# Issuing the expert weights of a mixture-of-experts stage from SyncE and ScalarE instead of GpSimd

## The chip, the cores and the metric

The kernel runs on one core of a Trainium2 chip, all in float32. The metric is the device time in microseconds of one execution. It computes one inference step of a decoder layer for a prompt of 512 tokens and a group of 8 samples, 520 tokens in all. Names of engines: PE is TensorE (PEld its weight load), DVE is VectorE, ACT is ScalarE, POOL is GpSimd, SP is SyncE.

## The reference

The layer is: adaLN norm, one input projection, four parallel token mixers, merge, output projection, residual; then a second norm and a mixture of experts. Only the last part matters here:

```python
def moe_ffn(h, lp):                       # x2: (520, 1024)
    scores = sigmoid(x2 @ w_router)       # 64 experts
    # group-limited choice: 4 of 8 groups, then the best 8 experts of a token
    gate = scores[idx] / sum * 2.5
    out = sum over the 8 chosen e of gate_e * swiglu(x, w_gate[e], w_up[e], w_down[e])
    out += swiglu(x, w_sh_gate, w_sh_up, w_sh_down)      # shared expert

def swiglu(x, wg, wu, wd):                # wg, wu (1024, 256), wd (256, 1024)
    return (silu(x @ wg) * (x @ wu)) @ wd
```

Each of the three matrices of an expert is 1 MB, so the 64 experts are 201 MB that come from HBM once.

## The kernel before

Up to some 870 us the kernel does the mixers, the merge and the router. The expert stage begins there and ends at about 1500 us; then the eight rows of each token are read back and added.

**Items, lanes and blocks.** The rows that go to one expert are cut into items of 64 rows. The items, in order of expert, are dealt to six lanes in six consecutive runs. A round `p` takes one item of each lane, and a block `(p, q)`, q = 0 to 2, takes those of lanes 2q and 2q+1: 128 rows, one half with the weights of one expert, the other with those of another. Here there are 16 rounds and so 48 blocks and 96 lane places. If a lane's item has the same expert as its item before, the weights in the lane's buffer are used again and not loaded.

**Buffers.** Each lane has one buffer for gate and up (`wgu`, 2 MB) and one for down (`wdn`, 1 MB), so a block's weights are loaded over those of the block three before. The rows of a block go to `xg[q]`, three buffers too.

**TensorE's order** (`block`, L2569) is: `gate_up` of block i (32 matmuls recorded on L2541), `down` of block i-1 (16, L2566), the transposes of block i's middle rows (2, L2551). `gate_up` waits for the semaphore `wg{q}` to reach 64 for each round (four transfers of 16), and `down` for `wd{q}` to reach 32 for each.

**ScalarE's order** (`block`, L1234): silu of the gate half (L1211), its half of the result copy of block i-1 to `ybuf` (L1224), and the copy of the turned middle rows, `hmT` (L1232), which `down` of block i needs. VectorE multiplies gate and up (L1900), turns the gathered rows of block i+2 into columns (L1917), and copies the other half of the result (L1927).

**GpSimd's order** (`steady`, L856) is one list per block: copy two columns of the order table (L788) after `gu_done` says that the product three blocks before the target is over; issue four indirect gathers of gate and up for block i-1 (`load_gate_up`, L768, recorded on L765); copy four more columns; gather the rows of block i (L779); issue two indirect gathers of down for block i-2 (`load_down`, L774); wait for the result of block i-5 and scatter it to HBM (L783). All eight go into one software queue, `q0`. The index of a weight gather is a row number for each of the 128 partitions, and a lane that needs no load has numbers beyond the bounds check, so that its rows are skipped while the semaphore still counts.

**The first blocks** are written out by hand (L817 to L850), because the buffers of the first six lanes come free one after the other as the stage before ends: some waits (`x1_out`, `sh_gu`, `sh_out0`, `sh_out1`, `sh_y`) stand between the loads.

**SyncE** loads and stores for the rest of the kernel; in the expert stage it stores the five shared-expert results (L598) and then waits for the end, when it loads the results back (L615 on, `early_load`).

Of the kernel before, what the change touches and what calls it, by code (L numbers as in the profile page):

```python
# [18 lines left out]
P = 128  # L19
# [120 lines left out]
def trunk(nc, A, O):  # L140
# [13 lines left out]
    yd = nc.dram_tensor("expert_rows", (TOK * TOPK, D), F32, kind="Internal").ap()  # L154

    with ExitStack() as ctx:
# [189 lines left out]
        last_p = view(TAB + 294, [1], 1, dt=I32)  # L346

# [60 lines left out]
        def rows(t):  # L408
            return P if t < NT else NS
# [8 lines left out]
        def _(sp):  # L418
            def load(dst, src, s):
                sp.dma_start(dst, src).then_inc(sem[s], 16)  # L420
# [181 lines left out]
            for t in range(TILES):  # L602
                sp.wait_ge(sem["sh_row"], t + 1)
                load(shared[t * P:t * P + rows(t), :], sh[t][0:rows(t), :], sh_stored[t])

            sp.wait_ge(sem["r_ready"], 1)
            last = sp.value_load(last_p, min_val=LAST_MIN - 1, max_val=MAXP - 2) + 1
            sp.wait_ge(sem["r_ready"], 3)
# [43 lines left out]
        def _(pool):  # L652
# [109 lines left out]
            w_rows = [A[name][0].rearrange("e (p c) n -> (e p) (c n)", p=P) for name in ("w_exp_gate", "w_exp_up", "w_exp_down")]  # L762

            def weight_rows(dst, src, index, s):
                pool.indirect_dma_start(out=dst, out_offset=None, in_=src, bounds_check=NE * P - 1, oob_is_err=False,  # L765
                                        in_offset=bass.IndirectOffsetOnAxis(ap=index, axis=0)).then_inc(sem[s], 16)

            def load_gate_up(q, at, lanes=range(2)):  # L768

                for lane in lanes:  # L770
                    for m in range(2):
                        weight_rows(wgu[2 * q + lane][:, m, :, :].rearrange("p c n -> p (c n)"), w_rows[m], at[:, lane:lane + 1], f"wg{q}")

            def load_down(q, at, lanes=range(2)):  # L774
                for lane in lanes:
                    weight_rows(wdn[2 * q + lane].rearrange("p c n -> p (c n)"), w_rows[2], at[:, 3 + lane:4 + lane], f"wd{q}")

# [8 lines left out]
            def order_part(p, q, lo, hi):  # L786
                pool.sem_inc(sem["x_col"], 1)
                pool.tensor_copy(order[q][:, lo:hi], orders.rearrange("p s n -> p (s n)")[:, bass.ds(p * 18 + (6 * q + lo), hi - lo)]).then_inc(sem["pool_chain"], 1)  # L788

            def gate_up_order(p, q):  # L790

                pool.wait_ge(sem["gu_done"], p * 3 + q - 3)
                order_part(p, q, 0, 2)
                pool.wait_ge(sem["pool_chain"], p * 6 + (n0 + 2 * q + 1))
                pool.sem_inc(sem["x_col"], 1)

            def rest_order(p, q, end=0):

                i = p * 3 + q
                if end < 3:  # L800
                    pool.wait_ge(sem["x_t"], i - 2)
                pool.wait_ge(sem["dn_done"], i - 4)
                pb, qb = block_at(p, q, -5)
                if later(pb):
                    pool.wait_ge(sem[f"yst{qb}"], pb * 16)
                order_part(p, q, 2, 6)
                pool.wait_ge(sem["pool_chain"], p * 6 + (n0 + 2 * q + 2 - end))
                pool.sem_inc(sem["x_col"], 1)
# [11 lines left out]
            load_gate_up(0, row[1])  # L820
            load_down(0, row[2])
            pool.wait_ge(sem["x1_out"], 16 * (TILES + 2))
            load_gate_up(1, row[2], range(1))
            pool.wait_ge(sem["sh_gu"], TILES)
            load_gate_up(1, row[2], range(1, 2))
            load_down(1, row[3], range(1))
# [4 lines left out]
            load_down(2, row[4], range(1, 2))  # L831
            pool.wait_ge(sem["sh_out0"], 32)
            pool.wait_ge(sem["sh_out1"], 16)
            load_gate_up(2, row[3], range(1))
            pool.wait_ge(sem["sh_y"], TILES)
            load_down(1, row[3], range(1, 2))
            load_gate_up(2, row[3], range(1, 2))
            load_down(2, row[4], range(1))
            pool.wait_ge(sem["x_t"], 1)
            block_gather(0, row[3])  # L840
            pool.wait_ge(sem["x_t"], 2)
            block_gather(1, row[4])
            pool.wait_ge(sem["gu_done"], 1)
            load_gate_up(0, row[4])
            pool.wait_ge(sem["x_t"], 3)
            block_gather(2, row[5])
            pool.wait_ge(sem["gu_done"], 2)
            load_gate_up(1, row[5])
            pool.wait_ge(sem["dn_done"], 1)
            load_down(0, row[5])  # L850
            n0 = step.n - 12
# [4 lines left out]
            def steady(p):  # L856
                for q in range(3):
                    gate_up_order(p, q)
                    load_gate_up(block_at(p, q, -1)[1], order[q])
                    rest_order(p, q)  # L860
                    block_gather(q, order[q])
                    load_down(block_at(p, q, -2)[1], order[q])
                    block_scatter(result_ready(p, q), order[q])
# [4 lines left out]
            for k in range(5):  # L868
                p, q = block_at(last, k, 3)
                if k == 0:  # L870
                    gate_up_order(p, q)
                    load_gate_up(block_at(p, q, -1)[1], order[q])
                rest_order(p, q, end=k)
                if k < 2:
                    load_down(block_at(p, q, -2)[1], order[q])
                block_scatter(result_ready(p, q), order[q])
# [3 lines left out]
        def _(act):  # L880
# [283 lines left out]
            def sh_result(t):  # L1164
                act.wait_ge(sem["sh_y"], t + 1)
                if t == 2:
                    act.wait_ge(sem["sh_out0"], 16)
                if t == 3:
                    act.wait_ge(sem["sh_out1"], 16)
                    act.wait_ge(sem["x1_out"], 16 * (TILES + 2))  # L1170
                for m in range(2) if t < NT else ():
                    last = act.copy(sh[t][:, m * 512:(m + 1) * 512], bank[SH_BANK[t][m]][:, :])
                for j in range(4) if t == NT else ():
                    last = act.copy(sh[t][0:NS, j * 256:(j + 1) * 256], bank[SH_BANK[t][0]][32 * j:32 * j + NS, 0:256])
                last.then_inc(sem["sh_row"], 1)

# [57 lines left out]
            def block(p, q):  # L1234
                gate(p, q)
                result_half(*block_at(p, q, -1))
                middle(p, q)
# [16 lines left out]
            for q in range(3):  # L1254
                block(last, q)
# [25 lines left out]
        def _(dve):  # L1281
# [556 lines left out]
            lanes = bank[7][:, 0:LANES * MAXP].rearrange("p (s n) -> p s n", n=2)  # L1838
            ts_(orders[:, 1:MAXB + 1, 0:2], lanes, pcol, float(MISS), ALU.add, ALU.add)
# [832 lines left out]
```

## Time and profile before

| | us |
|---|---|
| median of 3 runs | 1546.57 (1544.44 to 1548.23) |
| the profiled execution | 1549.48, its span 1547.7 |
| PE busy (share of span) | 1448.5 (94%) |
| DVE busy | 942.6 (61%) |
| POOL busy | 519.5 (34%) |
| ACT busy | 331.0 (21%) |
| q0, the software queue | 303.29 MB, 50.3% of 16 engines' span |
| q1, SyncE's queue | 122.39 MB, 22.8% |
| q10, ScalarE's queue | 10.65 MB, 1.8% |

The busy time of an engine is the sum of its instructions; waiting, register work and the issue of transfers from SP and ACT are not in it, while GpSimd's indirect gathers are. The DMA share is the mean busy share of the 16 transfer engines; where packets overlap it can pass 1. In the rows below, the number in brackets after a duration is the idle time before the instruction and what ended it. A matmul's end is modelled, so a busy PE isn't PE at its peak.

### The profile page before, as it was taken

How to read it: one execution, taken by the hardware profiler on the slowest of the kernel's cores; microseconds unless marked ns; L12 is line 12 of the kernel's file. 1: busy time of each engine (PE TensorE's matmuls, PEld its weight loads, DVE VectorE, ACT ScalarE, POOL GpSimd, SP SyncE). 2: the span in 40 equal slices, each digit the busy share in tenths (PEclk: the TensorE clock that was granted, in tenths of full speed). 3: DMA queues.
4: the chain of work that ended last, by engine and by line, in shares of the span. 5: the costliest groups of instructions: out<-in, count | busy, mean ns of one | idle time of the engine just before them, and what ended most of it. 6: DMA issues, size and time to landing. Idle time of an engine off the chain costs nothing.

```text
span 1547.7 us, 21472 instructions
## 1 busy us (share of the span) xinstructions
PE 1448.5 (94%) x7942; PEld 780.6 (50%) x7942; DVE 942.6 (61%) x1815; ACT 331.0 (21%) x628; POOL 519.5 (34%) x593
## 2 busy tenths in 40 slices
PE   4999999999999999999999999897999897999897
PEld 3444446777688768778644553232333332333333
DVE  4899992333231467436647937565776675776647
ACT  4111133332353323341223110010011010111020
POOL 2232100111000003200001236676676676666720
PEclk9999999999899899899999999998999998999999
DMA  9798735787512558828501499999999999999996
GB/s 342 257 321 297 269 108 219 267 293 266 190 49 82 166 190 284 277 84 287 188 29 57 153 363 420 415 418 417 402 390 392 372 413 416 418 345 367 406 390 281
DMA packets 138583, 437.31 MB, mean 283 GB/s; under 512 B 31526, under 2 KB 59546, under 8 KB 103678
## 3 DMA queue, kind: packets, MB, share of 16 engines
q0 software_dynamic: 65088, 303.29, 50.3%
q1 hardware_dynamic: 68080, 122.39, 22.8%
q10 hardware_dynamic: 5344, 10.65, 1.8%
q8 instruction: 49, 0.80, 0.2%
q14 instruction: 22, 0.18, 0.0%
HBM read 507.52 MB, written 45.61 MB: 357 GB/s over the span
## 4 chain that ended last, share of the span: by engine, by line
PE 69%; DMA 12%; issue 6%; DVE 6%; POOL 4%; ACT 2%; POOLq 0%; SPq 0%; ACTq 0%; DVEq 0%
PE bank L2150 15%; PE bank L2061 12%; PE bank L2541 11%; DMA arena<-in_w_exp_up_dram,arena 7%; PE bank L2566 4%; PE bank L2381 4%; PE bank L2369 4%; POOL arena L765 3%; DMA arena<-h_rows,arena 2%; PE bank L2183 2%; DVE arena L1917 1%; PE bank L2407 1%; DMA arena<-expert_rows 1%; PE bank L2611 1%; PE bank L2168 1%
## 5 line engine op out<-in xcount | busy, mean ns | idle before, releaser
L1917 DVE STREAM_TRANSPOSE arena<-arena 32x256 f32<-32x256 f32 x736 | 322.3, 438 | 123.0 <-DMA arena<-h_rows,arena 112.7
L2541 PE MATMUL bank<-arena 128*64 128x512 f32 x1536 | 354.1, 613 | 42.0 <-DMA arena<-in_w_exp_up_dram,arena 41.1
L2150 PE MATMUL bank<-arena 128*128 128x260 f32 x1024 | 242.1, 392 | 0.0
L2541 PEld LDWEIGHTS bank<-arena 128*64 128x64 f32 x1536 | 110.4, 138 | 250.4 <-issue 246.0
L2150 PEld LDWEIGHTS bank<-arena 128*128 128x128 f32 x1024 | 195.0, 194 | 35.3 <-ACT arena L1001 2.7
L2061 PE MATMUL bank<-arena 128*128 128x512 f32 (+1 forms) x448 | 190.8, 582 | 0.0
L2566 PE MATMUL bank<-arena 128*64 128x512 f32 x768 | 173.1, 592 | 1.1 <-DVE arena L1943 0.6
L2061 PEld LDWEIGHTS bank<-arena 128*128 128x128 f32 x448 | 83.8, 190 | 98.5 <-issue 91.0
L765 POOL DMA_INDIRECT arena<-in_w_exp_gate_dram,arena x96 | 97.8, 1019 | 98.2 <-POOL arena L788 38.0
L2566 PEld LDWEIGHTS bank<-arena 128*64 128x64 f32 x768 | 55.5, 136 | 110.2 <-issue 108.0
L765 POOL DMA_INDIRECT arena<-in_w_exp_up_dram,arena x96 | 96.1, 1001 | 30.7 <-issue 30.7
L765 POOL DMA_INDIRECT arena<-in_w_exp_down_dram,arena x96 | 95.2, 992 | 31.8 <-issue 27.9
L750 POOL TENSOR_TENSOR arena<-arena 128x1024 f32<-128x1024 f32 x8 | 25.4, 3177 | 229.4 <-ACT arena L1091 229.4
L1211 ACT ACTIVATE arena<-bank 128x256 f32<-128x256 f32 x48 | 18.5, 386 | 373.9 <-PE bank L2541 373.9
L736 POOL DMA_INDIRECT arena<-in_cache_sb_v_dram,arena x32 | 30.0, 937 | 174.3 <-PE bank L2183 103.8
L736 POOL DMA_INDIRECT arena<-in_cache_sb_k_dram,arena x32 | 32.4, 1013 | 137.4 <-DVE arena L1418 103.9
L1418 DVE TENSOR_TENSOR arena<-arena,bank 128x2048 f32<-128x2048 f32 x32 | 73.3, 2290 | 6.2 <-PE bank L2091 5.1
L758 POOL COPY arena<-arena 128x1024 f32<-128x1024 f32 (+1 forms) x5 | 10.1, 2024 | 194.7 <-DVE arena L1391 194.7
L1420 DVE TENSOR_REDUCE arena<-arena 128x32 f32<-128x2048 f32 x32 | 73.2, 2289 | 1.1
L2369 PE MATMUL bank<-arena 128*128 128x260 f32 x288 | 63.6, 382 | 2.6 <-DVE arena L1721 1.9
L1900 DVE TENSOR_TENSOR arena<-arena,bank 128x256 f32<-128x256 f32 x48 | 20.3, 423 | 74.1 <-ACT arena L1211 73.5
L1001 ACT ACTIVATE arena<-bank,arena 128x260 f32<-128x260 f32 x64 | 30.4, 478 | 160.9 <-PE bank L2150 160.5
(473 smaller groups left out, 1708.9 us busy)
## 6 DMA issues: line engine op xcount, KB each, us to landing
arena<-in_w_ada_dram SPq DMA_DIRECT2D x24, 1024.0 KB, 7.5
arena<-in_w_merge_gate_dram SPq DMA_DIRECT2D x16, 1024.0 KB, 6.5
arena<-expert_rows SPq DMA_DIRECT2D x16, 1024.0 KB, 13.4
arena<-in_w_in_dram SPq DMA_DIRECT2D x6, 2048.0 KB, 15.1
gate_logits<-arena ACTq DMA_DIRECT2D x32, 260.0 KB, 4.9
arena<-gate_logits SPq DMA_DIRECT2D x8, 1040.0 KB, 6.6
arena<-in_cache_swa_k_dram SPq DMA_DIRECT2D x24, 192.0 KB, 6.0
arena<-in_cache_swa_v_dram SPq DMA_DIRECT2D x24, 192.0 KB, 3.4
```

The costliest lines, as they stand in the source:

```text
L736: pool.indirect_dma_start(out=dst, out_offset=None, in_=src, in_offset=bass.IndirectOffsetOnAxis(ap=idx_kv[:, b, c:c + 1], axis=0)).then_i ...
L765: pool.indirect_dma_start(out=dst, out_offset=None, in_=src, bounds_check=NE * P - 1, oob_is_err=False, in_offset=bass.IndirectOffsetOnAxi ...
L1418: tt_(bs_prod, key_slot[n % 3], q, ALU.mult).then_inc(sem["kvk_used"], 1)
L1420: step(dve.tensor_reduce(bs_z[:, b, 8 * c:8 * c + 8, :], bs_prod.rearrange("p r (h d) -> p r h d", d=HD), AX, ALU.add))
L1917: ins = dve.transpose(xT[q][32 * n:32 * n + 32, :, 32 * r:32 * r + 32], src)
L2061: last = mm(bank[k % 2][:, 0:w], hT[:, c, cols(t)], src[:, c, 0:w], start=(c == 0), stop=(c == KC - 1))
L2150: last = mm(o[:, 0:HALF], gate_place(q)[:, c, ms], hT[:, c, row_half[u % 2]], start=(c == 0), stop=(c == KC - 1))
L2183: last = mm(bank[BS_BANK[b // 2]][j:j + BH, b % 2 * BW:b % 2 * BW + BW], bs_w[:, b, 8 * c + r, :], chunk[:, r, :], start=(c == 0 and r < 4 ...
L2369: last = mm(o, w[:, c, ms], oT[:, BR_AT[br] + c, part], start=(c == 0), stop=(c == BR_K[br] - 1))
L2381: last = mm(o[:, :], mT[:, c, cols(t)], src[:, c, :], start=(c == 0), stop=(c == KC - 1))
L2541: ins = mm(bank[gu_bank[q]][r, :].rearrange("p (g n) -> p g n", g=2), xT[q][:, c, r], wgu[2 * q + lane][:, :, c, :], start=(c == 0), stop= ...
L2566: ins = mm(bank[5 + m][r, :], hmT[q][:, c, r], wdn[2 * q + lane][:, c, m * 512:(m + 1) * 512], start=(c == 0), stop=(c == 1))
```

## The change

The conditional copy takes the place of the indirect gather for all weights. The table has one more row, `expert_p`: for each lane and round the number of its expert, or 128 where nothing is to be loaded. An engine reads one number into a register, takes it modulo 64 for the address, and copies 128 rows of 8 KB under the condition that it is below 64. SyncE issues gate and up (and, for the first three blocks, down), ScalarE issues down from block 3 on, inside its block, and the stores of the shared rows. GpSimd keeps the gathers and scatters of rows. `order[q]` needs one copy per block instead of two. The buffers and TensorE's and VectorE's orders are the same, except for one more VectorE operation that writes `expert_p`.

```diff
+    w_expert = [A[name][0].rearrange("e (p c) n -> e p (c n)", p=P) for name in ("w_exp_gate", "w_exp_up", "w_exp_down")]
+        expert_p = view(TAB + 298, [LANES * MAXP], 1, dt=I32)
 @blk.sync
-            for t in range(TILES):
-                sp.wait_ge(sem["sh_row"], t + 1)
-                load(shared[t * P:t * P + rows(t), :], sh[t][0:rows(t), :], sh_stored[t])
+            def gate_up_lanes(cell, b, lanes=range(2)):
+                for lane in lanes:
+                    e = sp.value_load(expert_p[:, bass.ds(cell + lane, 1)], min_val=0, max_val=MISS // P)
+                    for m in range(2):
+                        dst = wgu[2 * b + lane][:, m, :, :].rearrange("p c n -> p (c n)")
+                        sp.dma_start(dst.unsqueeze(1), w_expert[m][bass.ds(e % NE, 1)].rearrange("e p n -> p e n"), cond=e < NE).then_inc(sem[f"wg{b}"], 16)
+            def down_lanes(cell, b, lanes=range(2)):
...
+            def gate_up_load(p, q):
+                sp.wait_ge(sem["gu_done"], p * 3 + (q - 2))
+                sp.sem_inc(sem["x_col"], 1)
+                gate_up_lanes(p * 6 + 2 * q, q)
             sp.wait_ge(sem["r_ready"], 1)
             last = sp.value_load(last_p, min_val=LAST_MIN - 1, max_val=MAXP - 2) + 1
+            gate_up_lanes(0, 0)
+            down_lanes(0, 0)
+            sp.wait_ge(sem["x1_out"], 16 * (TILES + 2))
+            gate_up_lanes(2, 1, range(1))
+            sp.wait_ge(sem["sh_gu"], TILES)
+            gate_up_lanes(2, 1, range(1, 2))
+            down_lanes(2, 1, range(1))
+            sp.wait_ge(sem["r_ready"], 2)
+            down_lanes(4, 2, range(1, 2))
+            sp.wait_ge(sem["sh_out0"], 32)
+            sp.wait_ge(sem["sh_out1"], 16)
+            gate_up_lanes(4, 2, range(1))
+            sp.wait_ge(sem["sh_y"], TILES)
+            down_lanes(2, 1, range(1, 2))
+            gate_up_lanes(4, 2, range(1, 2))
+            down_lanes(4, 2, range(1))
+            with sp.Fori(1, last + 1) as p:
+                for q in range(3):
+                    gate_up_load(p, q)
 @blk.gpsimd
...
             def steady(p):
                 for q in range(3):
-                    gate_up_order(p, q)
-                    load_gate_up(block_at(p, q, -1)[1], order[q])
                     rest_order(p, q)
                     block_gather(q, order[q])
-                    load_down(block_at(p, q, -2)[1], order[q])
                     block_scatter(result_ready(p, q), order[q])
 @blk.scalar
                 last.then_inc(sem["sh_row"], 1)
+                act.wait_ge(sem["sh_row"], t + 1)
+                act.dma_start(shared[t * P:t * P + rows(t), :], sh[t][0:rows(t), :]).then_inc(sem[sh_stored[t]], 16)
...
+            def down_load(p, q):
+                for lane in range(2):
+                    e = act.value_load(expert_p[:, bass.ds(p * 6 + (2 * q + lane), 1)], min_val=0, max_val=MISS // P)
+                    act.dma_start(wdn[2 * q + lane].rearrange("p c n -> p (c n)").unsqueeze(1), w_expert[2][bass.ds(e % NE, 1)].rearrange("e p n -> p e n"), cond=e < NE).then_inc(sem[f"wd{q}"], 16)
-            def block(p, q):
+            def block(p, q, load=True):
                 gate(p, q)
                 result_half(*block_at(p, q, -1))
+                if load:
+                    down_load(*block_at(p, q, 2))
                 middle(p, q)
 @blk.vector
             lanes = bank[7][:, 0:LANES * MAXP].rearrange("p (s n) -> p s n", n=2)
+            ts_(expert_p, bank[7][0:1, 0:LANES * MAXP], 1.0 / P, float(MISS // P), ALU.mult, ALU.add)
```

## Rows read from the trace of the kernel before

**Rows 1.** Windows; us, busy of PE, PEld, DVE, ACT, POOL, clock, DMA share, GB/s.

```profile
932.00:1112.00 180.00, 160.89 (x710) 53.12 (x708) 114.05 (x255) 17.46 (x42) 118.36 (x140) 0.95 1.02 417
1112.00:1184.00 72.00, 72.00 (x334) 23.95 (x332) 55.01 (x124) 8.73 (x21) 50.05 (x60) 1.00 0.98 381
1184.00:1220.00 36.00, 31.15 (x138) 10.94 (x136) 20.45 (x46) 2.88 (x7) 24.20 (x29) 0.95 1.02 419
1220.00:1244.00 24.00, 23.61 (x110) 8.55 (x108) 17.77 (x40) 3.04 (x8) 16.84 (x21) 1.00 0.91 332
1244.00:1364.00 120.00, 108.21 (x480) 36.09 (x478) 76.24 (x170) 11.54 (x29) 82.18 (x99) 0.96 1.02 418
1364.00:1412.00 48.00, 48.00 (x221) 15.87 (x218) 37.97 (x86) 5.39 (x14) 33.68 (x40) 1.00 0.90 322
1412.00:1460.00 48.00, 44.58 (x198) 14.86 (x199) 29.97 (x67) 4.98 (x12) 33.65 (x40) 0.96 1.02 413
1460.00:1484.00 24.00, 22.95 (x106) 7.67 (x102) 16.85 (x37) 3.36 (x8) 14.87 (x18) 1.00 1.00 390
```

**Rows 2.** Waits, 820 to 1500 us; releaser, us, times, longest.

```profile
PE bank L2541 <- DMA arena<-in_w_exp_up_dram,arena: 41.1, 14, 6.4
```

**Rows 3.** Timeline of TensorE; start us, us, engine, line, operation.

```profile
1254.68 7.10 PE L2541 MATMUL bank<-arena 128*64 128x512 f32 x32
1261.61 3.60 PE L2566 MATMUL bank<-arena 128*64 128x512 f32 x16
1265.58 7.10 PE L2541 MATMUL bank<-arena 128*64 128x512 f32 x32
...
1281.16 8.79 PE L2541 MATMUL bank<-arena 128*64 128x512 f32 x32 [4.61 <-DMA arena<-in_w_exp_up_dram,arena]
```

**Rows 4.** Timeline of GpSimd, one iteration.

```profile
1258.68 0.19 POOL L788 COPY arena<-arena 128x2 int32 x1
1259.75 1.04 POOL L765 DMA_INDIRECT arena<-in_w_exp_gate_dram,arena  x1 [0.89 <-POOL arena L788]
...
1263.69 0.99 POOL L765 DMA_INDIRECT arena<-in_w_exp_up_dram,arena  x1 [0.30 <-issue]
...
1270.69 0.19 POOL L788 COPY arena<-arena 128x2 int32 x1
```

**Rows 5.** DMA queues, 870 to 1500 us; packets, MB, share.

```profile
q0 software_dynamic: 55007, 235.06, 93.8%
```

**Rows 6.** The window of 12 us with the highest rate.

```profile
1424.00:1436.00 12.00, 10.10 (x48) 3.28 (x44) 7.54 (x17) 1.25 (x3) 8.40 (x10) 1.00 1.02 425
```

**Rows 7.** DMA queues, 1486 to 1492 us.

```profile
q1 hardware_dynamic: 463, 1.84, 76.9%
q0 software_dynamic: 464, 0.52, 24.5%
```

**Rows 8.** By line, issues and register loads; ns min/median/max.

```profile
L420 SPq DMA_DIRECT2D arena<-in_w_ada_dram x24: 367/508/4169, 3.2 to 640.5; - x24
...
L1004 ACTq DMA_DIRECT2D gate_logits<-arena x32: 325/326/383, 270.1 to 686.5; - x32
...
L1203 ACTq TENSOR_LOAD <-arena x1: 481/481/481, 913.2 to 913.2; - x1
L1203 ACTq FUSED_REGOPS  x1: 180/180/180, 913.7 to 913.7; - x1
```

**Rows 9.** Timeline of ScalarE, copies of one block.

```profile
1265.34 0.59 ACT L1224 COPY arena<-bank 128x512 f32<-128x512 f32 x1 [3.05 <-PE bank L2566]
1265.82 0.38 ACT L1232 COPY arena<-bank 128x256 f32<-128x256 f32 x1
```

**Rows 10.** By line, line 1839 on DVE.

```profile
L1839 DVE TENSOR_SCALAR arena<-bank,arena x1: 356/356/356, 872.5 to 872.5; 128x132 int32<-128x132 f32 x1
```

**Rows 11.** Timeline of TensorE, the first two products that waited.

```profile
972.26 7.10 PE L2541 MATMUL bank<-arena 128*64 128x512 f32 x32 [0.33 <-DMA arena<-in_w_exp_up_dram,arena]
...
989.59 9.63 PE L2541 MATMUL bank<-arena 128*64 128x512 f32 x32 [6.36 <-DMA arena<-in_w_exp_up_dram,arena]
```

More of the change, by code:

```diff
@@ L599, in _ @@
                 load(x1d[t * P:t * P + rows(t), :], xr[0:rows(t), t, :], "x1_out")
-            for t in range(TILES):
-                sp.wait_ge(sem["sh_row"], t + 1)
-                load(shared[t * P:t * P + rows(t), :], sh[t][0:rows(t), :], sh_stored[t])
+            def gate_up_lanes(cell, b, lanes=range(2)):
[5 more added lines that the diff above has]
+            def down_lanes(cell, b, lanes=range(2)):
+                for lane in lanes:
+                    e = sp.value_load(expert_p[:, bass.ds(cell + lane, 1)], min_val=0, max_val=MISS // P)
+                    sp.dma_start(wdn[2 * b + lane].rearrange("p c n -> p (c n)").unsqueeze(1), w_expert[2][bass.ds(e % NE, 1)].rearrange("e p n -> p e n"), cond=e < NE).then_inc(sem[f"wd{b}"], 16)
+            def gate_up_load(p, q):
+                sp.wait_ge(sem["gu_done"], p * 3 + (q - 2))
+                sp.sem_inc(sem["x_col"], 1)
+                gate_up_lanes(p * 6 + 2 * q, q)
             sp.wait_ge(sem["r_ready"], 1)
             last = sp.value_load(last_p, min_val=LAST_MIN - 1, max_val=MAXP - 2) + 1
+            gate_up_lanes(0, 0)
[17 more added lines that the diff above has]
+                    gate_up_load(p, q)
             sp.wait_ge(sem["r_ready"], 3)
@@ L760, in _ @@
                 step(pool.memset(xg[q], 0.0))
[L762 to L776, printed above, removed]
             def block_gather(q, at):
@@ L784, in block_scatter @@
                                         in_offset=None, bounds_check=TOK * TOPK - 1, oob_is_err=False).then_inc(sem[f"yst{q}"], 16)
[L786 to L795, printed above, removed]
             def rest_order(p, q, end=0):
@@ L801, in rest_order @@
                     pool.wait_ge(sem["x_t"], i - 2)
-                pool.wait_ge(sem["dn_done"], i - 4)
                 pb, qb = block_at(p, q, -5)
@@ L805, in rest_order @@
                     pool.wait_ge(sem[f"yst{qb}"], pb * 16)
-                order_part(p, q, 2, 6)
-                pool.wait_ge(sem["pool_chain"], p * 6 + (n0 + 2 * q + 2 - end))
+                pool.sem_inc(sem["x_col"], 1)
+                pool.tensor_copy(order[q][:, 2:6], orders.rearrange("p s n -> p (s n)")[:, bass.ds(p * 18 + (6 * q + 2), 4)]).then_inc(sem["pool_chain"], 1)
+                pool.wait_ge(sem["pool_chain"], p * 3 + (n0 + q + 1))
                 pool.sem_inc(sem["x_col"], 1)
@@ L819, in _ @@
             last = pool.value_load(last_p, min_val=LAST_MIN - 1, max_val=MAXP - 2) + 1
[L820 to L826, printed above, removed]
             pool.wait_ge(sem["r_ready"], 2)
@@ L830, in _ @@
                 block_gather(q, row[q])
[L831 to L851, printed above, removed]
+            for q in range(3):
+                pool.wait_ge(sem["x_t"], q + 1)
+                block_gather(q, row[3 + q])
+            n0 = step.n - 6
             pool.wait_ge(sem["y_a"], 1)
@@ L869, in _ @@
                 p, q = block_at(last, k, 3)
-                if k == 0:
-                    gate_up_order(p, q)
-                    load_gate_up(block_at(p, q, -1)[1], order[q])
                 rest_order(p, q, end=k)
-                if k < 2:
-                    load_down(block_at(p, q, -2)[1], order[q])
                 block_scatter(result_ready(p, q), order[q])
@@ L1254, in _ @@
             for q in range(3):
-                block(last, q)
+                block(last, q, load=q < 1)
             for t in range(3):
```

## The prediction

> **What bounds the kernel now.** I read the granted clock and span first, then the busy shares of the expert stage in stretches, then what TensorE waits for there, then one iteration of GpSimd and of TensorE side by side, and last the DMA queues.
>
> The stretches [rows 1] cover the expert stage, 932 to 1484 us. In the long ones at 932 to 1112 and 1244 to 1364 us the DMA column is 1.02, that is full, at 417 and 418 GB/s, and there PE is busy only 160.89 of 180 and 108.21 of 120 us. In the stretches between (1112, 1220, 1364) PE is busy for all or nearly all of the time and the DMA share is 0.90 to 0.98. So the stage changes between two states: transfers bound it, or TensorE does. TensorE's only large wait is for expert weights, 41.1 us in 14 waits [rows 2]; it is blamed on the up matrices because these are issued last of a gate-and-up set. A wait costs more than itself: the gate-and-up product after a wait of 4.61 us takes 8.79 us where the one before took 7.10 [rows 3].
>
> GpSimd looks like a third bound, and it is the one that the change goes for. From one order copy to the same copy of the next block it takes 1270.69 - 1258.68 = 12.01 us, each issue about 0.99 us with a gap of 0.30 [rows 4]. TensorE's block takes 1265.58 - 1254.68 = 10.90 us [rows 3]. When TensorE isn't held up, GpSimd falls behind by 1.1 us per block. The gate-and-up set issued from 1259.75 on is for the product that starts at 1281.16; its buffers were free when the product three before it ended, one block of 10.90 before 1261.61, that is at 1250.7. So it was issued 9 us late.
>
> But being late matters only where the transfer engines run dry. In the whole stage they are short of 1.02 by 72 x 0.04 + 24 x 0.11 + 48 x 0.12 + 24 x 0.02 = 2.9 + 2.6 + 5.8 + 0.5 = 11.8 us [rows 1], 11.6 us of full transfer. That, not the 50 us that 1.1 us over 46 blocks suggests, is the ceiling on what faster issue can give.
>
> **The change part by part.**
>
> *GpSimd loses six of eight issues per block and one of its two order copies.* 6 x 1.29 + 2 us goes from its loop of 12.0 us, which leaves some 3 us; GpSimd is no longer near a bound. What it can give is the 11.6 us above. Lower bound of the gain 0 (if the dry spells were full buffers, since TensorE is at full rate in them), upper 11.6. I take 11.6, as a lateness of 9 us is close to a whole block's worth of prefetch. The late next thing is then a transfer or a full buffer.
>
> *Skipped lanes send nothing.* 64 experts fill 96 lane places, so 32 of the 96 loads of each matrix carry no rows. The software queue still shows 55,007 packets for 235.06 MB [rows 5]; 384 transfers of 128 rows and 16 endings would be 55,296, so skipped rows are packets too, 96 x 144 = 13,824 of them. Price: with a full DMA share the rate is 417 to 418 GB/s over long stretches [rows 1] and 425 in the best twelve microseconds [rows 6]. 1.7% of the 384 us in the four full stretches is 6 us if all the difference is small packets; 13,824 are some 60% of them. I take 4 us, bounds 0 and 6.
>
> *Weights move from one queue into two, beside the rows in a third.* Before, one software queue held everything in order of issue, and that is the order of use: gate and up of block i, then down of block i-1, and so on. Now SyncE's queue has gate and up, ScalarE's has down, GpSimd's has rows. How do queues share the engines? In 1486 to 1492 us, where SyncE's queue and GpSimd's both had work, they got through 463 and 464 packets, though one moved 1.84 MB and the other 0.52 [rows 7]: turns, packet by packet. Down and gate/up rows are both 8 KB, so down gets as much as gate and up together while it has work. When TensorE waits for gate and up of block i, the down weights of i-1, i and i+1 have been issued (each as soon as the product three blocks earlier is done). Those of i-1 are wanted next in any case; those of i and i+1 used to stand behind. They are up to 4 loads, on average 4 x 64/96 = 2.7; one is 1.049 MB at 417 GB/s = 2.51 us [rows 1]. So TensorE waits 6.7 us longer (10 at most), once for each time that the transfers become the bound again. Within such a stretch it isn't paid twice, since what ran ahead needn't be loaded later; but in the slack stretch after it nothing is bought with the lead, as both buffers are full there. There are four such entries: 932, 1184, 1244 and 1412 us [rows 1]. 4 x 6.7 = 27 us. Lower bound 0 (the lead is fully used), upper 4 x 10 = 40. I take 27.
>
> The Trainium skill says, in "DMA: Bandwidth & Descriptors", section "Queues, rings and completion order", that each DMA engine goes round the queue rows that have work, one packet at a time. The counts 463 and 464 agree. By a plain first-in-first-out over all queues this term would be 0 and the sum would come out as a gain.
>
> *ScalarE's new work in the block.* Between its half of the result copy and the copy of the turned middle rows it now issues two down loads. Nearest rows on ScalarE: a register load 481 ns, register arithmetic 180 ns, a DMA issue 326 ns [rows 8]; together 2 x 0.99 = 2.0 us, perhaps 3 with more arithmetic for the remainder and the condition. Queued behind it are the copy of the middle rows and then the next silu. The copy starts at 1265.82 now, and TensorE needs it only for the down product that follows the gate-and-up product of 1265.58 [rows 9], 6.9 us after that start (1272.5). Moved by 2 to 3 us it ends before 1269.3: cost 0. Lower bound 0; the upper bound is a rival below.
>
> *SyncE's new work* is four issues and two register loads per block. SyncE otherwise sits through the stage, and its loop ends before the product of block last x 3 + 1 that its next wait wants, so the final loads aren't late. Cost 0.
>
> *Start.* The table of experts adds one DVE operation before the first loads; the nearest, on 132 values of all partitions, is 0.36 us [rows 10]. SyncE's issue at 0.4 us instead of 1.3 gives back about as much at once, and the loads are limited by freed buffers here. ScalarE's five stores add 5 x 0.33 = 1.6 us to it before block 0; the gathers no longer wait behind weights. I take 0, bounds -3 and +2.
>
> *Sum.* -11.6 - 4 + 27 + 0 = +11 us, against the profiled execution's own 1549.48 us (span 1547.7) 1560.5. The median of the runs shown is 2.9 us lower, so 1557.5 us; I predict 1557.5. The tail after the stage (stores of the last rows, their loads, the final sums) is the same work and moves with it.
>
> **The rivals.**
>
> *Issue was the bound and order doesn't matter.* The down weights that run ahead are bytes that must come anyway; if the later dry spells absorb the lead, only the gains are left: -11.6 - 4 = -16, from the median 1531 us. For it: GpSimd is back to back at 12.01 us in both kinds of stretch. Against it: the two longest waiting stretches are at a full DMA share. Chance 0.22.
>
> *Bytes alone decide.* Same bytes, same engines, same rate: queues only permute them, gain of relief and loss of order cancel, 1546 us. The Trainium skill has this as a rule: in "DMA: Bandwidth & Descriptors", section "Issuing engines are not separate DMA queues", it says that issuing from several engines saves only the issuing time, usually little. Where I differ is that 11.6 us of idle transfer time is there to be saved, and that order costs. Chance 0.13.
>
> *ScalarE is held in its issue.* SyncE's issue of an earlier load took up to 4.17 us against a median of 0.51 [rows 8], which is an engine held while its queue is full. If that hits both of ScalarE's issues, 2 x 4.17 + 1.3 = 9.6 us passes before the middle copy, 2.8 us more than the 6.9 us it has [rows 9]; over the 33 blocks or so of full transfers that is +90 us, 1640 us. Against it: it took a backlog of short rows, and ScalarE's own 32 issues never took over 0.39 us. It begins to cost from 3.2 us per issue. Chance 0.04.
>
> *The change doesn't skip.* If a conditional copy whose condition fails still moved its rows, 96 more loads of 2.51 us would be 241 us. The condition is there to prevent that; chance 0.01.
>
> **How the numbers follow.** My forecast has 0.60. Its own range is 1548 to 1571 (order term 17 to 40, the rest as taken). To hold eight in ten the range must reach into the first rival: 1533 to 1573. No change can be told within about 0.3%, 4.6 us. Slower: most of the 0.60, and the last two rivals, 0.62; faster: the first rival and a part of the second, 0.25; same 0.13.
>
> **What would show it.** The rows of GpSimd's weight gathers are gone, and its loop waits for others. TensorE waits for gate/up weights fewer but longer times, one of them within the first five blocks, where the only one now is of 0.33 us [rows 11]. The down transfers land sooner after issue than the gate and up ones. DMA share in the slack stretches no higher than now. ScalarE's copy of the middle rows starts 2 to 3 us later and no one waits for it. The prediction is wrong if TensorE's waits for weights total less than 41.1 us; wrong in the other way if down products wait, or middle copies.

## The result, and the profile after

| | before | after |
|---|---|---|
| median of 3 runs, us | 1546.57 (1544.44 to 1548.23) | 1569.38 (1561.88 to 1574.65) |
| the profiled execution, us | 1549.48 | 1561.88 |
| expert stage, start of the first gate-and-up product to end of the last down product | 917.57 to 1500.2 = 582.7 | 915.32 to 1514.4 = 599.1 |
| from there to the end of the span | 47.5 | 45.7 |

The changed kernel is slower, ratio 1.0128 [1.0092, 1.0163]. Its profiled execution is the fastest of its three; a second one (1568.45 us, below) has a stage of 601.5 us. In these profiles all that is lost is lost in the expert stage: the start of the stage and the tail give back 2.3 and 1.8 us.

The page's line of busy times: GpSimd, which was busy for 519.5 us, now has 222.5.

```profile
PE 1444.5 (93%) x7942; PEld 776.0 (50%) x7942; DVE 939.6 (60%) x1816; ACT 334.9 (21%) x629; POOL 222.5 (14%) x262
```

Windows of after, columns as in [rows 1]. The stretches with a full DMA share are still there. The one at 1220 to 1244 is new in kind: the share falls to 0.61 and TensorE isn't busy throughout either.

```profile
932.00:1112.00 180.00, 153.70 (x684) 50.98 (x682) 111.78 (x253) 18.45 (x41) 30.11 (x40) 0.92 1.00 409
1112.00:1184.00 72.00, 72.00 (x334) 24.07 (x332) 51.35 (x116) 8.82 (x20) 15.66 (x21) 1.00 0.97 385
1184.00:1220.00 36.00, 24.83 (x116) 8.14 (x110) 23.87 (x54) 3.65 (x8) 6.71 (x9) 0.89 1.02 420
1220.00:1244.00 24.00, 22.37 (x94) 7.28 (x96) 9.66 (x22) 1.73 (x4) 2.24 (x3) 0.88 0.61 223
1244.00:1364.00 120.00, 107.03 (x476) 35.59 (x474) 77.43 (x175) 13.06 (x29) 21.16 (x28) 0.94 0.99 405
1364.00:1412.00 48.00, 46.70 (x216) 15.76 (x214) 33.34 (x75) 5.38 (x12) 9.70 (x14) 1.00 0.92 351
1412.00:1460.00 48.00, 43.44 (x190) 14.27 (x188) 32.12 (x72) 5.38 (x12) 9.42 (x13) 0.93 1.00 410
```

Waits of TensorE for gate and up in the stage (870 to 1520 us), against 41.1 us in 14 [rows 2]:

```profile
PE bank L2529 <- DMA arena<-in_w_exp_up_dram: 57.4, 11, 12.8
```

The waits themselves, in TensorE's timeline. The four longest, 10.19 to 12.80 us, are 1.6 to 2 times before's longest of 6.4 us. The first of them, of 11.74 us, stands before the fifth block; before had no wait there, 0.33 us before the sixth block and 6.36 before the seventh [rows 11].

```profile
972.46 9.19 PE L2529 MATMUL bank<-arena 128*64 128x512 f32 x32 [11.74 <-DMA arena<-in_w_exp_up_dram]
...
1064.27 9.36 PE L2529 MATMUL bank<-arena 128*64 128x512 f32 x32 [11.89 <-DMA arena<-in_w_exp_up_dram]
...
1197.86 7.10 PE L2529 MATMUL bank<-arena 128*64 128x512 f32 x32
...
1221.63 9.19 PE L2529 MATMUL bank<-arena 128*64 128x512 f32 x32 [12.80 <-DMA arena<-in_w_exp_up_dram]
...
1303.61 9.16 PE L2529 MATMUL bank<-arena 128*64 128x512 f32 x32 [10.19 <-DMA arena<-in_w_exp_up_dram]
...
1453.43 9.34 PE L2529 MATMUL bank<-arena 128*64 128x512 f32 x32 [4.57 <-DMA arena<-in_w_exp_up_dram]
```

What went on before the wait that ends at 1221.63: the DMA queues from 1196 to 1208 us. The three queues got through 306, 303 and 297 packets. Down (q10) moved 2.18 MB, as much as gate and up together (q1, 2.20 MB), although a block needs twice as much of these. In four more windows of 12 us, from 944, 1040, 1280 and 1436 us, the two weight queues are within about 2% of each other as well (at most 300 against 294 packets). The software queue's count says less: in one_queue below it is 288 beside 609, twice the 144 packets of one transfer of rows, so the 297 here may be all that it had to move.

```profile
q1 hardware_dynamic: 306, 2.20, 44.0%
q10 hardware_dynamic: 303, 2.18, 43.5%
q0 software_dynamic: 297, 0.67, 14.3%
```

SyncE had issued the transfers as soon as their buffers were free. The set that the product of 1221.63 waits for was issued from 1184.28 to 1187.11 us, right behind the product three blocks before, and landed some 34 us later:

```profile
1184.28 0.34 SPq L610 DMA_DIRECT2D arena<-in_w_exp_gate_dram  x1
...
1186.72 0.39 SPq L610 DMA_DIRECT2D arena<-in_w_exp_up_dram  x1
```

Most of the issues took 0.33 to 0.38 us each. By line, ScalarE's and SyncE's, columns as in [rows 8]. A copy whose condition fails takes 0.07 to 0.10 us: of SyncE's 192 issues 64 are that short, as many as the lanes that load nothing (2 x 32).

```profile
L1216 ACTq TENSOR_LOAD <-arena x90: 272/282/304, 938.2 to 1489.3; - x90
...
L1217 ACTq DMA_DIRECT2D arena<-in_w_exp_down_dram x90: 90/344/416, 939.1 to 1490.2; - x90
...
L610 SPq DMA_DIRECT2D arena<-in_w_exp_gate_dram x96: 73/333/358, 871.8 to 1476.1; - x96
...
L610 SPq DMA_DIRECT2D arena<-in_w_exp_up_dram x96: 73/377/1327, 872.3 to 1476.3; - x96
```

ScalarE's timeline of one block: the middle copy (L1211) starts 2.52 us after the result copy, where it was 0.48 us [rows 9].

```profile
1175.74 0.59 ACT L1203 COPY arena<-bank 128x512 f32<-128x512 f32 x1 [3.05 <-PE bank L2554]
1176.72 1.44 ACTq L1217 DMA_DIRECT2D arena<-in_w_exp_down_dram  x2
1178.26 0.37 ACT L1211 COPY arena<-bank 128x256 f32<-128x256 f32 x1 [1.93 <-issue]
```

GpSimd's timeline now has waits in it, and its loop takes what TensorE's block takes: 1178.22 - 1167.49 = 10.7 us from scatter to scatter, against 12.01 back to back [rows 4].

```profile
1167.49 1.02 POOL L803 DMA_INDIRECT expert_rows<-arena  x1 [5.73 <-DVE arena L1915]
1170.61 0.18 POOL L815 COPY arena<-arena 128x4 int32 x1 [2.09 <-DVE arena L1905]
1171.75 1.03 POOL L799 DMA_INDIRECT arena<-h_rows,arena  x1 [0.96 <-POOL arena L815]
1178.22 1.02 POOL L803 DMA_INDIRECT expert_rows<-arena  x1 [5.44 <-DVE arena L1915]
```

### The profile page after: what moved, and what is told of

The parts are those of the page before. It is cut to its first block, busy times and chain, and to the rows that moved or that the text cites. A ratio compares the mean times of both kernels' runs of the same rounds, so it can differ in the third digit from the quotient of the medians.

```text
span 1560.1 us, 22255 instructions
## 1 busy us (share of the span) xinstructions
PE 1444.5 (93%) x7942; PEld 776.0 (50%) x7942; DVE 939.6 (60%) x1816; ACT 334.9 (21%) x629; POOL 222.5 (14%) x262
## 3 DMA queue, kind: packets, MB, share of 16 engines
q1 hardware_dynamic: 86784, 260.77, 44.6%
q0 software_dynamic: 23616, 101.90, 17.7%
q10 hardware_dynamic: 14288, 73.60, 11.8%
## 4 chain that ended last, share of the span: by engine, by line
PE 75%; DMA 16%; DVE 3%; ACT 2%; SPq 1%; issue 1%; ACTq 0%; DVEq 0%
PE bank L2529 16%; PE bank L2138 14%; DMA arena<-in_w_exp_up_dram 14%; PE bank L2049 12%; PE bank L2554 6%; PE bank L2369 4%; PE bank L2357 4%; PE bank L2171 2%; PE bank L2599 2%; PE bank L2395 1%; PE bank L2156 1%; PE bank L2145 1%; DMA arena<-in_w_in_dram 1%; DMA arena<-in_w_ada_dram 1%; PE bank L2051 1%
## 5 line engine op out<-in xcount | busy, mean ns | idle before, releaser
L2529 PE MATMUL bank<-arena 128*64 128x512 f32 x1536 | 354.6, 614 | 58.3 <-DMA arena<-in_w_exp_up_dram 57.4
L1905 DVE STREAM_TRANSPOSE arena<-arena 32x256 f32<-32x256 f32 x736 | 321.9, 437 | 10.1
L2138 PE MATMUL bank<-arena 128*128 128x260 f32 x1024 | 237.4, 387 | 0.0
L2138 PEld LDWEIGHTS bank<-arena 128*128 128x128 f32 x1024 | 191.8, 191 | 33.8 <-ACT arena L978 2.7
L2049 PEld LDWEIGHTS bank<-arena 128*128 128x128 f32 x448 | 83.5, 189 | 97.7 <-issue 90.3
L803 POOL DMA_INDIRECT expert_rows<-arena x48 | 49.0, 1020 | 349.8 <-DVE arena L1915 341.9
L799 POOL DMA_INDIRECT arena<-h_rows,arena x48 | 49.6, 1033 | 119.1 <-DVE arena L1867 52.0
L2357 PE MATMUL bank<-arena 128*128 128x260 f32 x288 | 63.6, 382 | 2.6 <-DVE arena L1708 1.9
L2369 PE MATMUL bank<-arena 128*128 128x512 f32 x128 | 60.4, 631 | 0.0
L2357 PEld LDWEIGHTS bank<-arena 128*128 128x128 f32 x288 | 54.3, 189 | 11.6 <-issue 2.3
L1203 ACT COPY arena<-bank 128x512 f32<-128x512 f32 x48 | 28.2, 587 | 146.0 <-PE bank L2554 146.0
```

Of the source, the lines that this page charges most:

```text
L799: pool.indirect_dma_start(out=xg[q], out_offset=None, in_=h2d, bounds_check=TOK - 1, oob_is_err=False, in_offset=bass.IndirectOffsetOnAxis ...
L803: pool.indirect_dma_start(out=yd, out_offset=bass.IndirectOffsetOnAxis(ap=at[:, 5:6], axis=0), in_=ybuf[q], in_offset=None, bounds_check=T ...
L1905: ins = dve.transpose(xT[q][32 * n:32 * n + 32, :, 32 * r:32 * r + 32], src)
L2049: last = mm(bank[k % 2][:, 0:w], hT[:, c, cols(t)], src[:, c, 0:w], start=(c == 0), stop=(c == KC - 1))
L2138: last = mm(o[:, 0:HALF], gate_place(q)[:, c, ms], hT[:, c, row_half[u % 2]], start=(c == 0), stop=(c == KC - 1))
L2357: last = mm(o, w[:, c, ms], oT[:, BR_AT[br] + c, part], start=(c == 0), stop=(c == BR_K[br] - 1))
```

## The experiments

Times are medians in us. The first five rows shared one chip and 23 runs of the kernel before, the other three a second chip and 11 runs. "Stage" and "tail" are of each profiled execution, measured as in the table above; where the stage starts, by code that is the same up to there but for the first loads, varies from 913.28 to 920.80 us.

| kernel | median (lowest to highest) | ratio to before | stage | tail |
|---|---|---|---|---|
| before, first chip | 1549.43 (1545.18 to 1554.61) | | 582.7 | 47.5 |
| changed_again | 1569.82 (1563.96 to 1572.92) | 1.0130 [1.0108, 1.0151] | 601.5 | 45.7 |
| one_queue | 1547.89 (1544.16 to 1555.12) | 0.9995 [0.9981, 1.0009] | 573.6 | 55.7 |
| down_one_block_ahead | 1549.94 (1548.76 to 1558.90) | 1.0014 [1.0000, 1.0029] | 586.6 | 47.3 |
| down_alone_moved | 1563.36 (1559.20 to 1566.15) | 1.0089 [1.0072, 1.0106] | 600.2 | 45.9 |
| before, second chip | 1550.08 (1547.25 to 1557.10) | | | |
| one_queue_late | 1581.63 (1577.72 to 1586.29) | 1.0198 [1.0172, 1.0224] | 611.0 | 57.1 |
| one_queue_early_tail | 1542.40 (1538.90 to 1543.37) | 0.9940 [0.9917, 0.9962] | 574.6 | 46.2 |
| changed_more_act | 1569.16 (1565.04 to 1574.39) | 1.0120 [1.0092, 1.0148] | 605.9 | 46.4 |

(The first row's stage and tail are of the profile shown before the prediction.) In the cuts of the edits below, "..." stands for lines left out.

My theory was that of the prediction: turns between queues let down weights overtake gate and up weights that are wanted sooner. The rivals were that the cost comes from another part of the change (ScalarE's issues, conditional copies as such, a late start), and that bytes alone decide.

**changed_again**: the changed kernel once more, without an edit.

> The changed kernel once more, so that the others stand beside it on the same chip. By all theories 15 to 23 us above the kernel before, with four or five waits of TensorE for gate/up weights of 10 us or more.

It is as slow as in the first measurement, and the waits have the same sum and number: 57.8 us in 11, the longest 12.0. How they are spread isn't the same: two are of 10 us or more, where four or five were expected, and the next are of 6.28, 5.86 and 4.74 us. So a single long wait isn't a property of the kernel; the sum is, and in part the sum over a stretch (below).

```profile
1067.34 9.29 PE L2529 MATMUL bank<-arena 128*64 128x512 f32 x32 [10.70 <-DMA arena<-in_w_exp_up_dram]
...
1227.81 9.27 PE L2529 MATMUL bank<-arena 128*64 128x512 f32 x32 [12.03 <-DMA arena<-in_w_exp_up_dram]
```

**one_queue**: all weights on SyncE's queue in the old order of use, down of block i-1 behind gate and up of block i. The last two lines of the cut are ScalarE's.

```diff
+            def down_after(p, q):
+                sp.wait_ge(sem["dn_done"], p * 3 + (q - 2))
...
+                down_lanes(p * 6 + 2 * q, q)
...
                 for q in range(3):
                     gate_up_load(p, q)
+                    down_after(*block_at(p, q, -1))
+            down_after(last, 2)
...
-                if load:
-                    down_load(*block_at(p, q, 2))
```

> The down loads of block 3 on go from ScalarE's queue to SyncE's, each set behind the gate/up set of the next block: one hardware queue in the order of use, all else as in the changed kernel. Theory 'order' (down weights run ahead because each queue gets its turn): the long waits of 10 us go, the waits for gate/up fall from 57 us to 25 to 40, and the time falls by 20 to 35 us against the changed kernel, to 1535 to 1547, as the gain of prompt issue is then left alone. Theory 'issue on ScalarE' (register loads and issues between its copies hold the block): also faster, but the waits that go are those of down products or middle copies, not those for gate/up. Theory 'hardware queues move weights more slowly': no change, 1562 to 1575.

Windows of one_queue: in the first, 417 GB/s where after has 409; the slack stretch 1364 to 1412 isn't full here either, with TensorE busy 48.00 of 48 us.

```profile
932.00:1112.00 180.00, 162.02 (x714) 53.48 (x712) 115.33 (x260) 17.44 (x42) 32.35 (x43) 0.95 1.01 417
1112.00:1184.00 72.00, 72.00 (x334) 23.96 (x332) 53.85 (x121) 8.73 (x21) 13.75 (x19) 1.00 1.00 402
...
1364.00:1412.00 48.00, 48.00 (x222) 16.00 (x220) 36.38 (x82) 5.85 (x14) 9.97 (x13) 1.00 0.92 355
...
1460.00:1484.00 24.00, 24.00 (x114) 7.87 (x110) 9.54 (x22) 2.50 (x6) 2.33 (x4) 1.00 0.71 271
```

TensorE's waits of one_queue in the stage and just behind it:

```profile
PE bank L2539 <- DMA arena<-in_w_exp_up_dram: 30.9, 8, 6.8
PE bank L2609 <- DMA arena<-expert_rows: 7.9, 1, 7.9
```

Its DMA queues from 1196 to 1208 us: one queue of weights takes 88.4%, where two shared 44.0 and 43.5% in after.

```profile
q1 hardware_dynamic: 609, 4.42, 88.4%
q0 software_dynamic: 288, 0.61, 13.1%
```

The waits fall from 57.4 to 30.9 us and the stage by 25.5 us (27.9 against changed_again), with the same kind of copies, the same bytes and an idle GpSimd. So the order costs, and conditional copies as such don't. The waits are in the range expected, the fall of 21.9 us too; the time is just above the 1547 that was its upper end, and the median is only that of before: the stage is 9.1 us shorter than before's, and the tail 8.2 us longer. That wait of 7.9 us is for the result rows of the last blocks, which SyncE loads; SyncE's timeline shows why they come late. It stands in the last down set until 1464.98 us and issues the first result load at 1466.74, though the product that this load waits for in the code (of block 45) was over at about 1459.

```profile
1452.77 12.21 SPq L615 DMA_DIRECT2D arena<-in_w_exp_down_dram  x4
1466.74 2.74 SPq L423 DMA_DIRECT2D arena<-expert_rows  x4
```

**one_queue_early_tail**: the same, but the last down set is issued by ScalarE, so that SyncE isn't held. The cut is against one_queue: the first line is SyncE's, the others are ScalarE's, and `block(last, 0)` alone has load=True.

```diff
-            down_after(last, 2)
...
-            def block(p, q, load=True):
+            def block(p, q, load=False):
...
+                if load:
+                    down_load(*block_at(p, q, 2))
```

> As one_queue, but ScalarE issues the very last down set, so that SyncE needn't wait for its buffer before it starts the loads of the results. In one_queue the stage ends 11 us earlier than before and the time hardly moves; its first result load was issued some 7 us after the product that frees its buffer. Theory 'the tail is bound by its 20 MB of loads, and SyncE started them late': 4 to 7 us less than one_queue, 1541 to 1544, and under the kernel before. Rival 'the tail waits for the scatters of rows': no change, 1547.

SyncE's timeline: the first result load now follows right behind that product, at 1465.76, in an execution whose stage is 6 us later on the clock of the span (it ends at 1495.4 instead of 1489.1).

```profile
1459.10 1.38 SPq L615 DMA_DIRECT2D arena<-in_w_exp_down_dram  x2
1465.76 2.08 SPq L423 DMA_DIRECT2D arena<-expert_rows  x4
```

TensorE's waits:

```profile
PE bank L2540 <- DMA arena<-in_w_exp_up_dram: 33.9, 9, 6.8
...
PE bank L2610 <- DMA arena<-expert_rows: 0.3, 1, 0.3
```

The tail is back at 46.2 us and the kernel takes 1542.40 us, in the range expected: 0.6% less than before on the same chip, and by the ratios to before 0.55% less than one_queue. This is the version to keep.

**down_one_block_ahead**: the changed kernel, with down issued one block before its use instead of two.

```diff
-                    down_load(*block_at(p, q, 2))
+                    down_load(*block_at(p, q, 1))
...
-                block(i // 3, i % 3)
+                block(i // 3, i % 3, load=i > 1)
...
-                block(last, q, load=q < 1)
+                block(last, q, load=q < 2)
```

> ScalarE issues the down loads of block i+1 instead of i+2, so that they can run ahead by one block less; its queue, its work per block and its place in the block are the same. Theory 'order': the long waits shrink by about 3.3 us each (1.33 loads of 2.51 us), 10 to 15 us less in all, 1547 to 1558. Theory 'issue on ScalarE': no change, as it does the same work. Rival to both: down weights now come late, and TensorE waits at the down product.

Its waits:

```profile
PE bank L2529 <- DMA arena<-in_w_exp_up_dram: 47.8, 12, 12.6
...
PE bank L2554 <- DMA arena<-in_w_exp_down_dram: 0.3, 1, 0.3
```

Half the lead, and 20 us of changed_again's 20 come back in the median, more than the 10 to 15 that I had expected. All three queues are still in use here, so this part of the loss comes from the lead and not from their number. In the profiled executions the stage gives back 12.5 us against after and 14.9 against changed_again, about half of the order term; the rest of the difference is the start of the stage, 913.28 us against 915.32 and 919.53. Of the stage's gain the waits are 9.6 and 10.0 us, and the 48 gate-and-up products take 351.1 us in all, where they took 354.6 and 356.5. Three waits of 8 to 12.6 us are left. Why the median gains more than the stage does is open.

**down_alone_moved**: the kernel before, with only the down loads moved to SyncE (first three blocks) and ScalarE. Gate, up and rows stay on GpSimd, which loses two of its eight issues. The first line of the cut is GpSimd's, the others are ScalarE's.

```diff
-                    load_down(block_at(p, q, -2)[1], order[q])
...
+            def block(p, q, load=True):
...
+                if load:
+                    down_load(*block_at(p, q, 2))
```

> The kernel before with only the down loads moved (SyncE for the first three blocks, ScalarE after that); gate/up stay indirect gathers of GpSimd, in one queue with the rows, and GpSimd's loop falls from 12.0 to about 9.4 us, under TensorE's 10.9. Theory 'order': slower than before by 5 to 25 us although GpSimd is relieved, with waits for gate/up of 10 us. Theory 'hardware queues are slower for weights' would leave gate/up alone and give about half of the loss. Theory 'GpSimd's issue bounds the stage': faster than before, about 1535.

Its waits:

```profile
PE bank L2560 <- DMA arena<-in_w_exp_up_dram,arena: 54.3, 9, 9.7
```

This small part of the change has most of its loss: +14 us of 20 in the median and a stage of 600.2 us. Giving down a queue of its own is what costs; whether gate and up go by GpSimd or SyncE matters less (6.5 us between the two medians).

**one_queue_late**: one_queue with gate and up issued one block (10.9 us) later, to see what late issue is worth.

```diff
-                sp.wait_ge(sem["gu_done"], p * 3 + (q - 2))
+                sp.wait_ge(sem["gu_done"], p * 3 + (q - 1))
```

> One hardware queue in order of use, but gate and up of a block are issued only when the product two blocks before is done, not three: 10.9 us later, somewhat more than GpSimd's lateness of up to 9 us in the kernel before. Theory 'lateness runs the transfer engines dry' (my 11.6 us): the stage grows by 10 us or more against one_queue, back to the kernel before or beyond, 1555 to 1590, with DMA share well under 1 before each wait. Rival 'the dry spells were full buffers': within 3 us of one_queue.

Its windows: the DMA share is lower than in one_queue in six of the eight stretches, and TensorE is held even at 1112 to 1184 (68.53 of 72 us).

```profile
932.00:1112.00 180.00, 156.15 (x676) 52.11 (x672) 112.23 (x253) 17.47 (x42) 30.93 (x41) 0.93 0.98 398
1112.00:1184.00 72.00, 68.53 (x299) 22.56 (x300) 45.17 (x103) 6.70 (x17) 12.76 (x18) 0.95 0.89 340
...
1244.00:1364.00 120.00, 105.63 (x466) 35.66 (x462) 74.59 (x168) 11.61 (x28) 20.52 (x28) 0.94 0.93 372
...
1412.00:1460.00 48.00, 47.30 (x220) 15.85 (x218) 34.12 (x77) 5.38 (x13) 10.02 (x13) 1.00 0.93 357
```

TensorE's waits: 59.0 us in 17.

```profile
PE bank L2539 <- DMA arena<-in_w_exp_up_dram: 59.0, 17, 7.3
```

A whole block of lateness costs 611.0 - 573.6 = 37 us of stage: 28 us of waits, and 9 us in the gate-and-up products, 364.4 us in all against 355.7. The profiled execution is the slowest of its six; by the ratios of the medians it is 2.0% of 1550, 31 us. The share isn't short before every wait, as had been expected: from 1184 to 1244 it is 1.00 and 1.01, and one wait there is of 5.10 us. In these runs many shorter waits and a lower share go with late issue, and fewer, longer ones at a full share with the wrong order.

**changed_more_act**: the changed kernel, ScalarE delayed by two idle register loads before each down load.

```diff
                 for lane in range(2):
+                    for _ in range(2):
+                        act.value_load(expert_p[:, bass.ds(p * 6 + (2 * q + lane), 1)], min_val=0, max_val=MISS // P)
```

> The changed kernel with two idle register loads more for each down load on ScalarE, four per block, 2 us more between its copies. Theory 'order' and my step that ScalarE's work is hidden by the gate/up product: no change, 1565 to 1574. Theory 'ScalarE's work is part of the loss': 2 us over 45 blocks, up to 90 us more.

ScalarE's timeline: the middle copy starts 4.66 us after the result copy, 2.1 us later than in after.

```profile
1173.07 0.59 ACT L1203 COPY arena<-bank 128x512 f32<-128x512 f32 x1 [3.04 <-PE bank L2556]
1175.13 2.50 ACTq L1219 DMA_DIRECT2D arena<-in_w_exp_down_dram  x2
1177.73 0.37 ACT L1211 COPY arena<-bank 128x256 f32<-128x256 f32 x1 [4.08 <-issue]
```

The median is that of the changed kernel. The stage of the one profiled execution is 4 to 7 us longer, though its waits for weights have the same sum (57.2 us in 9): the 48 gate-and-up products take 361.7 us in all, where they took 354.6 and 356.5, and six timed runs don't bear this out as a loss. ScalarE's work is hidden with room to spare.

## Why the prediction was right, and where its size was off

The direction, the mechanism and the range held; the median is 1569.4 us where 1557.5 was predicted, +22.8 us (in the two later series +20.4 and +19.1) where +11 was. By its own steps:

*Order and turns, +27 us.* Measured 25.5 and 27.9 us of stage between one_queue and the two profiles of the changed kernel; by medians on one chip, changed_more_act less one_queue_early_tail, 1569.16 - 1542.40 = 26.8 us. The working was "once per entry, 6.7 us, four entries". TensorE's waits for weights, added up over the blocks behind each entry, in us:

| blocks | before | one_queue | after | changed_again |
|---|---|---|---|---|
| 0 to 17 | 18.6 | 17.4 | 25.8 | 26.9 |
| 18 to 28 | 5.2 | 2.7 | 12.8 | 12.0 |
| 29 to 41 | 11.8 | 10.8 | 14.3 | 15.6 |
| 42 to 47 | 5.6 | 0 | 4.6 | 3.3 |
| all | 41.1 | 30.9 | 57.4 | 57.8 |

Against one_queue the changed kernel waits 8.3, 10.1, 3.5 and 4.6 us longer in after, and 9.5, 9.3, 4.8 and 3.3 in changed_again: 6.6 and 6.7 us on average. So the first stretch, though after has two waits of over 11 us in it, is paid for about once, as the working said. The single entries aren't alike, from 3.3 to 10.1 us, so that the average comes so near to 6.7 is partly luck: two entries cost more than the mean of 2.7 loads ahead, two less. The sum is all wait: the 48 gate-and-up products take 354.6 us in after and 355.7 in one_queue. The lead isn't given back: behind the 12.80 us wait the DMA share is 0.61 with TensorE at work, and SyncE issues nothing between 1207.81 and 1231.95 us, where the next set loads nothing for either lane. The Trainium skill says ("DMA: Bandwidth & Descriptors", "Issuing engines are not separate DMA queues") that starting DMAs on several engines saves only the time that it takes to initiate them. In these runs that isn't all: by the order of the weights it also cost some 27 us. Its rule of turns between queues ("Queues, rings and completion order") agrees with the 306 and 303 packets of the two weight queues.

*GpSimd's relief, -11.6, and skipped lanes, -4 us.* This is the term that was mis-sized. Together they gave -9.1 us of stage in one_queue, -8.1 in one_queue_early_tail (574.6 against 582.7), and -7.7 in its median, not -15.6. The miss of 8 us here is what separates the +11 of the prediction from the +19 of the second chip; the 1 to 4 us more of the other two series stay open, and the spread of their runs is larger than that. The ceiling was reckoned as if every dry spell came from late issue. But with prompt issue, in one_queue, the stretch 1364 to 1412 still has a share of 0.92 (before 0.90 [rows 1]) with TensorE busy all the time. No issue is late there, so what is missing is a free buffer, which is what the prediction had named as its lower bound. one_queue_late shows that lateness does cost: 10.9 us of it in every block cost 31 to 37 us. GpSimd's, 9 us in the iteration read, cost 9 us at most, skipped lanes included, so the prefetch covered most of it. More than half of what was gained in waits lies behind block 42 (5.6 us to 0). How the 8 us split between relief and skipped lanes isn't shown. The small packets did go: under 512 B there are 22,410 in before and 8,450 in after, from 870 to 1500 us. But the rate hardly rose. Over the stretches that are full in before the mean is 417.0 GB/s there, 418.7 in one_queue_early_tail and 415.1 in one_queue; 0.4% of these 384 us would be 1.6 us, an estimate, and not 4. Twelve microseconds at a full share moved 420 to 422 GB/s in after, and 418 to 425 in before.

*ScalarE, 0.* Right: the copy moved by 2.04 us, TensorE waited for it once for 0.5 us, as it did before, and another 2.1 us changed nothing. In the stage its issues of down took at most 0.416 us, SyncE's of gate and up 1.327; the rival of a held queue didn't occur. Why not can be worked out from the start of the kernel before: each of SyncE's five issues of over 2 us in the first 200 us ended with 1,900 to 2,500 packets of its queue outstanding, and with up to 1,600 none took over 0.6 us (an estimate from the packets issued and done in that trace). ScalarE's three sets of down loads are 6 x 144 = 864 at most. The prediction's own threshold has a slip: 6.9 us less 1.3 for the registers leaves 2.8 us per issue, not 3.2. So does GpSimd's loop: 12.0 less 6 x 1.29 and 2 leaves 2.3 us, not 3; the three operations of it shown above take 2.2.

*SyncE and the start, 0.* Right within what can be read: the start of the stage moved by -2.3 us in one profile and +2.0 in the other. In the changed kernel SyncE's final loads weren't late (tail 45.7 us).

*The rivals.* "Issue was the bound" falls with down_alone_moved, where GpSimd is relieved too and the kernel is slower, and with the small relief. "Bytes alone decide" falls with one_queue against changed_again: same bytes, 22 us. Conditions that don't skip: the three queues moved 260.77 + 101.90 + 73.60 = 436.3 MB in the span, as they did before (122.39 + 303.29 + 10.65), and SyncE's and ScalarE's queues together 28,964 packets from 870 to 1500 us, where the 288 loads with none skipped would be 288 x 144 = 41,472.

*Signs.* GpSimd's weight gathers are gone and its loop waits; waits fewer (11 for 14) and longer; one of 11.74 us before the fifth block; total above 41.1 us; no wait for down, and none new for a middle copy: all as written, but that before's wait of 0.33 us stood before the sixth block and not within the first five. In changed_again the fifth block waits only 3.24 us and the fourth 5.86. The share in the slack stretches is no higher but for 0.92 against 0.90 at 1364 to 1412. The profile gives no landing times for conditional copies, so that down lands sooner is seen by the bytes per queue only.

Open: the three runs of the changed kernel spread over 0.8% (1561.88 to 1574.65), those of before over 0.2%; in the later, longer series it was 0.6% for both. That the expert rows' turns on GpSimd's queue cost something by themselves wasn't tried.

## What to carry to other kernels

Where transfers bound a stage, one queue in order of use is a schedule: in this kernel, moving the loads that are wanted later to a queue of their own let them overtake those that are wanted first, by as much as their buffers allowed. Move the whole order to another engine, or limit the lead of what is moved, and look at which other work stands behind the last issue of that engine. Before counting dry transfer time as a gain of prompter issue, see whether the consumer is at full rate there; here the buffers were full then, and the share rose only from 0.90 to 0.92.

## What the runs showed of the hardware

A conditional copy whose condition fails cost its engine 0.07 to 0.10 us and moved nothing; one that copies cost 0.33 to 0.38 us to issue, against 0.99 us and a gap of 0.30 for the indirect gather on GpSimd [rows 4]. The weights moved at the same rate by either kind of queue: in twelve microseconds at a full share 420 to 422 GB/s by the hardware queues in after, 418 to 425 by the software queue in before. Two queues with 8 KB rows got equal numbers of packets within about 2%, and so equal bytes, though one was wanted twice as much. TensorE's product after a wait of 4.6 to 12.8 us took 9.16 to 9.36 us in after instead of 7.10, with a mean granted clock of 0.77 in the one from 1221.7 to 1230.7 us, so these five waits cost 10.7 us more than themselves. one_queue's shorter waits cost as much in this way (its 48 products take no less time), so it is no part of the difference between the two.
